# One of two weight sums of the up projection: from an accumulating DMA to an addition on GpSimd

## The reference

```python
h = jnp.einsum('btd,df->btf', x, ffn_w_up)          # (tokens, 2048) @ (2048, 2 * 5504)
h, new_ffn = causal_dwconv(ffn_hist, h, ffn_conv_w, ffn_conv_b)   # 3 taps
hu, hg = jnp.split(h, 2, axis=-1)
f = jnp.einsum('btf,fd->btd', jax.nn.silu(hg) * hu, ffn_w_down)
x = layer_norm(ALPHA * x + f, ln2_g, ln2_b)
```

## Time and profile before

| | |
|---|---|
| runs | 2182.31 us median of 3 (2180.84 to 2182.39) |
| the profiled execution's own time | 2182.37 us |
| its span, first to last instruction | 2180.8 us |
| mean granted TensorE clock | 0.974 |
| busy: TensorE, VectorE, ScalarE, GpSimd | 95%, 64%, 41%, 21% |
| DMA | 296.86 MB, 136 GB/s over the span |

### The profile page before, as it was taken

One profiled execution on the slowest core, in us unless ns is written; L12 is line 12 of the kernel. 1 busy time (PEld: TensorE's weight loads), 2 busy tenths in 40 slices (PEclk: granted clock), 3 DMA queues, 4 the chain that ended last, 5 costly groups with the idle time before them and its releaser, 6 DMA issues.

```text
span 2180.8 us, 41649 instructions
## 1 busy us (share of the span) xinstructions
PE 2074.7 (95%) x16117; PEld 2047.7 (94%) x16125; DVE 1403.6 (64%) x1870; ACT 888.4 (41%) x1234; POOL 448.9 (21%) x558
## 2 busy tenths in 40 slices
PE   8999999789974999999999999999999999999995
PEld 8999999689973999999999999999999999999994
DVE  3788888565459777778777777777774222334324
ACT  4344443442225455545555454555453111222223
POOL 0112122133232222222121212211121000004222
PEclk9999999799995999999999999999999999999998
DMA  6322232022233767677676767676759323332222
GB/s 222 103 75 73 72 84 76 19 68 87 87 85 115 207 178 193 173 189 186 184 185 180 191 178 192 177 193 177 186 164 321 88 86 89 113 119 85 85 77 82
DMA packets 90615, 296.86 MB, mean 136 GB/s; under 512 B 11620, under 2 KB 12388, under 8 KB 90528
## 3 DMA queue, kind: packets, MB, share of 16 engines
q1 hardware_dynamic: 72384, 233.79, 33.9%
q0 software_dynamic: 16992, 59.87, 14.2%
q10 hardware_dynamic: 1152, 1.96, 0.2%
HBM read 271.61 MB, written 23.97 MB: 136 GB/s over the span
## 4 chain that ended last, share of the span: by engine, by line
PE 90%; DVE 5%; issue 2%; DMA 1%; ACT 1%; POOL 0%; SPq 0%; ACTq 0%; DVEq 0%; POOLq 0%
PE acc L750 40%; PE acc L804 22%; PE acc L498 22%; PE acc L507 2%; PE acc L594 1%; DVE comb L1588 1%; DMA sum<-w_up 1%; PE acc L583 1%; PE acc L574 1%; DVE resid L1801 0%; DVE resid L1584 0%; DVE w_lo L1556 0%; DVE acc L1473 0%; DMA raw_a<-w_down 0%; PE acc L570 0%
## 5 line engine op out<-in xcount | busy, mean ns | idle before, releaser
L750 PE MATMUL acc<-comb,w_hi 128*128 128x274 f32 x4816 | 931.2, 292 | 45.4 <-DVE w_lo L1556 28.3
L750 PEld LDWEIGHTS acc<-comb,w_hi 128*128 128x128 f32 x4816 | 767.6, 191 | 48.4 <-issue 31.8
L750 PE MATMUL acc<-comb,w_lo 128*128 128x274 f32 x2408 | 699.7, 291 | 0.0
L804 PE MATMUL acc<-acts,w_hi 128*128 128x272 f32 x2752 | 460.1, 289 | 5.6 <-DVE resid L1745 2.2
L750 PEld LDWEIGHTS acc<-comb,w_lo 128*128 128x128 f32 x2408 | 462.9, 192 | 0.0
L804 PEld LDWEIGHTS acc<-acts,w_hi 128*128 128x128 f32 x2752 | 390.3, 188 | 6.6 <-issue 3.5
L804 PE MATMUL acc<-acts,w_lo 128*128 128x272 f32 x1376 | 284.8, 288 | 0.0
L1065 ACT ACTIVATE w_hi<-sum 128x1024 fp32r<-128x1024 f32 x172 | 182.4, 1060 | 229.8 <-PE acc L750 124.7
L1556 DVE TENSOR_TENSOR w_lo<-sum,w_hi 128x1024 fp32r<-128x1024 f32 x172 | 211.7, 1231 | 90.6 <-ACT w_hi L1065 87.4
L1556 DVE TENSOR_TENSOR w_lo<-raw_a,w_hi 128x1024 fp32r<-128x1024 f32 x129 | 157.5, 1221 | 98.9 <-ACT w_hi L1065 98.9
L804 PEld LDWEIGHTS acc<-acts,w_lo 128*128 128x128 f32 x1376 | 216.4, 188 | 0.0
(11 more groups left out here) (226 smaller groups left out, 2661.1 us busy)
## 6 DMA issues: line engine op xcount, KB each, us to landing
raw_a<-w_up SPq DMA_DIRECT2D x129, 512.0 KB, 5.9
sum<-w_up SPq DMA_DIRECT2D x86, 512.0 KB, 3.6
sum<-w_up POOLq DMA_DIRECT2D x86, 512.0 KB, 7.6
stage<-w_stream SPq DMA_DIRECT2D x84, 512.0 KB, 3.6
sum<-w_down SPq DMA_DIRECT2D x45, 448.0 KB, 3.4
sum<-w_down SPq DMA_DIRECT2D x24, 512.0 KB, 3.6
act_spill<-prod_f SPq DMA_DIRECT2D x43, 272.0 KB, 6.4
act_raw<-act_spill POOLq DMA_DIRECT2D x43, 272.0 KB, 4.1
```

Of the source, the lines that this page charges most:

```text
L750: mm = pe.matmul(bank(BANK_OF[j]), wt[:, k * P:(k + 1) * P], comb[:, j, k, b, :], start=start and q == 0, stop=stop and q == 2, skip_group ...
L804: mm = pe.matmul(acc[:, a, h, 0:D_TOK // 2], wt[:, w * P:(w + 1) * P], x[:, h * (D_TOK // 2):(h + 1) * (D_TOK // 2)], start=start and q == ...
```

## The change

`sum_3` is now loaded by SyncE with quarter 2 (before: quarter 0), and GpSimd adds `raw_a11`, which holds quarter 0 of the same period, with a tensor_tensor from SBUF to SBUF in place of the accumulating DMA. Its semaphore now rises by 1 per period. GpSimd waits for `a11_in` too, and SyncE waits for `s3_summed` before it loads the next content into `raw_a11`.

```diff
             def load_s3(f):
-                sp.dma_start(sum_3[:, :], quarter(f, 0)).then_inc(s3_in, 16)
+                sp.dma_start(sum_3[:, :], quarter(f, 2)).then_inc(s3_in, 16)
...
             def up_loads(f, p):
 
                 sp.wait_ge(s2_made, f + 1)
+                sp.wait_ge(s3_summed, f + 1)
                 sp.wait_ge(up_lo, f * N_PROD + 1)
                 load_a11(f + 1)
...
             last = N_PROD * (FT - 1)
+            sp.wait_ge(s3_summed, FT)
             sp.wait_ge(s2_made, FT)
...
             def hi_s3(f, n):
-                act.wait_ge(s3_summed, f * 16 + 16)
+                act.wait_ge(s3_summed, f + 1)
                 up_hi_of(n, sum_3)
...
             pool.wait_ge(s3_in, 16)
-            pool.dma_start(sum_3[:, :], dram["w_up"][2], accum_op=ALU.add).then_inc(s3_summed, 16)
+            pool.wait_ge(a11_in, 16)
+            pool.tensor_tensor(sum_3[:, :], sum_3[:, :], raw_a11[:, :], ALU.add).then_inc(s3_summed, 1)
...
                 pool.wait_ge(s3_in, f * 16 + 16)
-                pool.dma_start(sum_3[:, :], quarter(f, 2), accum_op=ALU.add).then_inc(s3_summed, 16)
+                pool.wait_ge(a11_in, f * 16 + 16)
+                pool.tensor_tensor(sum_3[:, :], sum_3[:, :], raw_a11[:, :], ALU.add).then_inc(s3_summed, 1)
```

## The result

The changed kernel takes 2186.49 us (median of 20 runs, 2183.8 to 2190.4), the kernel before 2183.77 us (20 runs, 2180.84 to 2185.44). The ratio is 1.0016, taken of the means (2186.93 to 2183.50 us), 95% interval 1.001 to 1.0023: a small loss, under the 0.2% that the prediction took as its bound. The forecast was 2186.0.

A forecast was written before the change was run, and what follows sets the result against it. TensorE, busy 95% of the span and full in the up stage, was taken as the bound. Span 2180.8 + 3.9 (13 stalls of 0.3) - 0.3 = 2184.4, plus 1.57 us around it: 2186.0 us; range 2181 to 2197.

The forecast's parts named there:

- the 0.2% that the prediction took as its bound: Whole kernel: about 0.2%, 4.4 us, is what a measurement of it can tell from no change.
- TensorE is full in the stage, so nothing is won: Up stage: TensorE busy 860.00 of 860.00 us, so removing 43 accumulating DMAs is worth 0 there.
- The start of the stage, -0.3 us: Start of up stage: TensorE's 0.66 us wait for `u_two` may shrink with less DMA traffic; gain 0 to 0.66, taken 0.3.
- The addition, 2.34 us: GpSimd: each of 43 additions of 128 x 1024 float32 was taken as 2.34 us, delaying VectorE by its own length.
- both estimates from rows: GpSimd's addition, from the 548-column tensor_tensor: 2.50 us in proportion to columns, 2.34 us with a fixed part of 185 ns.
- Slack 2.02 us, stall 0.3: First period of a loop body: `u3` may end 2.02 us later before product 5; 2.34 us of delay stalls TensorE 0.3 us.
- Only the first periods, 13 times: Up stage: TensorE stalls only in each loop body's first period, after a table load; 13 x 0.3 = 3.9 us.
- The other periods, margin 0.20 to 0.27 us: Periods other than a body's first: `u3` still ends 0.20 to 0.27 us before its latest harmless end, so no stall.
- the margin breaks: Rival, other periods: an addition blocking from 2.54 us on stalls 28 more periods; 2199 us, far end 2264; chance 20%.
- The waits: SyncE's wait for `s3_summed` and GpSimd's for `a11_in`: claimed to hold up no load, cost 0.
- The sum, 2186.0 us: Whole kernel: span 2180.8 + 3.9 - 0.3 = 2184.4, plus 1.57 us around the span, gives 2186.0 us.
- The chances: Whole kernel: forecast 62%, hidden 14%, margin broken 20%, faster 3%, sum off DMA's path 1%; within 0.2%: 55%.

The follow-up runs named there:

- all ten: The ten profiled kernels: the kernel before, the changed kernel and eight experiments; the stage begins between 700.19 and 705.11 us in them.
- 256 columns: Changed kernel plus a GpSimd addition of 256 columns directly before the one of 1024: three periods 65.12 us, ratio to before 1.0055.
- the body of six: Changed kernel with six periods in ScalarE's loop body in place of three: three periods 64.26 and 64.56 us by turns, ratio to before 1.0017.
- memset: Changed kernel with a 2-column GpSimd addition and a 1632-column memset in place of the 1024-column addition: three periods 64.26 us, one execution.
- 768: Changed kernel with GpSimd adding only 768 of the 1024 columns: three periods 64.26 us, stage 900.11 us, one execution.
- addition behind `c22`: Changed kernel with the addition one step later in GpSimd's list, behind the copies that wait for `c22`: three periods 64.26 us, ratio to before 0.9999.
- addition on VectorE: Changed kernel with VectorE making the addition behind the low part of product 6, GpSimd only the first: three periods 64.26 us, ratio to before 1.0005.

## Why the prediction was right, step by step

- *TensorE is full in the stage, so nothing is won.* Right. Without the DMAs (DMA share 0.58) no version has three periods under 64.26 us behind the first body.
- *The start of the stage, -0.3 us.* The wait for `u_two` there did fall, from 0.66 to 0.34 us, and the first period is 0.30 us shorter, the figure taken. That it fell because of the change isn't shown. The time between the first two `p_one` copies is 22.39 us before and 22.09 after, but 21.76 us in the kernel with both accumulating DMAs and the added waits, and 21.76 to 22.41 among all ten.
- *The addition, 2.34 us.* VectorE was shut out for 2.21 us, 0.13 less than the value taken and so just below both estimates from rows. The fixed part of 185 ns, taken from the copy's record, is not part of the time in which VectorE is shut out: 256 columns cost 0.53 us, 2.1 ns a column with nothing on top. As the length of the addition itself 2.34 was close: its undisturbed record is 2.40 us. The sum took that length for the time shut out. The estimate of 2.25 us, half of the 4497 ns that the Trainium skill ("GPSIMD Engine Reference", section 3.1) has for 2048 columns, was nearer to the time shut out, but under the addition's own 2.40 us.
- *Slack 2.02 us, stall 0.3.* The slack was right: the gap of 0.20 us is 2.21 less 2.02, to 0.01. What the step missed is that a stall costs TensorE more than its gap: `u3` ended 0.13 us before the matmul, as read from the earlier trace rows, but that pair of matmuls takes 0.52 us where 0.42 is usual, 0.1 us more. The time shut out was taken 0.13 us too long and this 0.1 us was left out; the two errors cancelled, and 0.3 came out by some luck.
- *Only the first periods, 13 times.* Right: the stalls go with the table loads, in the body of three and in the body of six. 13 x 0.30 = 3.9 us was the stage's 3.89 us. That figure holds the start of the stage too: its first period is 0.30 us shorter than before, and the next is 0.55 longer, 0.25 more than a stall. So 12 bodies by 0.303 us, 3.64 us, are its clean part.
- *The other periods, margin 0.20 to 0.27 us.* Right in sign, too small in size. It is 0.63 us: `u3` ends at 1014.50, and 1015.26 - 0.13 would do. The low part there takes 3.01 us in place of 1.23, so it is 1.78 us late and not 2.01 or 2.07. `u3` ends only 1.65 us later, since before it began 0.13 us later behind `gated`. The prediction had the plain load of `sum_3` land when it did; GpSimd gets it earlier, 6.33 us after `p_one` (1009.55 less 1003.22) against 6.69 (1009.40 less 1002.71), so the addition starts as soon as `make_s4` ends. In the first periods that changes nothing, since `make_s4` ends later still. 0.53 us more in the experiment still caused no stall. The rival "the margin breaks" had a fifth of the chance; it needed 0.63 us more of blocking than there was, where the prediction had it at 0.20.
- *The waits.* Right, 0.
- *The sum, 2186.0 us.* It stands on one profile of before, 2182.37 us. The 20 runs of before have a median of 2183.77, and from there the same sum gives 2187.4, where 2186.49 was measured. Forecast was a rise of 3.6 us; it is 2.7 us by the medians and 3.4 by the means. So the hit within 0.5 us owes something to the base too.
- *The chances.* One result can't test them. It fell where the forecast stood, at 0.16%, just inside the bound of 0.2%, and its interval, 1.001 to 1.0023, crosses the bound.

## What to carry to other kernels

When work is moved to GpSimd, don't ask how busy VectorE is. Ask which of VectorE's two-input instructions stands beside GpSimd's read, what is queued behind it, and which of those TensorE waits for; then add the whole of GpSimd's instruction to that chain, less what idle time the chain has, and compare it with the slack. The cure is a place: one step later in GpSimd's list, or one swap in VectorE's, removed all of the cost. And where a loop has a repeated length, compare that: it showed 0.3 us in 64 us, in a single profile, where the whole time needed 20 executions of each kernel to show 0.16%.

## What the runs showed of the hardware

- GpSimd's memset of 1632 columns (1.46 us) ran beside a VectorE instruction with two SBUF inputs, which took its usual 1.22 us, while a 2-column addition of 0.81 us didn't end before such an instruction did. The Trainium skill ("SBUF — State Buffer", section "Who interferes with whom") says so, and the trace agrees.
- VectorE is shut out for 2.1 to 2.2 ns a column of GpSimd's addition, with no fixed part, at 256, 768 and 1024 columns.
- A wait of TensorE with a gap of 0.20 us cost 0.30 us: the first matmul came 0.13 us after the end of VectorE's instruction, and the first pair took 0.52 us in place of 0.42.
- With one accumulating DMA in two gone, plain DMAs to other tiles land sooner after their issue, in the medians: the loads of `raw_a` in 3.6 us where the page of before has 5.9, the spill of `gated`'s product in 2.2 where it has 6.4. In the three kernels that leave VectorE undelayed in these places (addition behind `c22`, memset, addition on VectorE) the loads take 4.4 us and the spill 3.3 to 3.5. That it is the later issue that makes the difference isn't shown. No engine waited for these DMAs between 740 and 1600 us in any kernel.
